# A decode step's recurrent states as the moving operand of their matmuls, with zero-padded queries as weights

## The reference, cut to what matters

```
def step(S, inp):
    qc, kc, vc, gc = inp
    b = jnp.cumsum(gc, axis=1)
    o = jnp.einsum('bthk,bhkv->bthv', qc * jnp.exp(b), S)
    ...
    bl = b[:, -1]
    S = jnp.exp(bl)[..., None] * S + jnp.einsum('bshk,bshv->bhkv', kc * jnp.exp(bl[:, None] - b), vc)
    return S, o
```

## Time and profile before

| | |
|---|---|
| three runs | 2344.84, 2345.38 (median), 2351.37 us |
| profiled execution, own time | 2343.79 us |
| its span in the profile | 2342.0 us |
| busy in the span: PE, PEld, DVE | 2258.5, 2182.4, 1586.0 us |
| busy in the span: ACT, POOL | 654.2, 1225.4 us |
| mean granted clock of TensorE | 0.975 |

### The profile page before, as it was taken

One profiled execution on the slowest core, in us unless ns is written; L12 is line 12 of the kernel. 1 busy time (PEld: TensorE's weight loads), 2 busy tenths in 40 slices (PEclk: granted clock), 3 DMA queues, 4 the chain that ended last, 5 costly groups with the idle time before them and its releaser, 6 DMA issues.

```text
span 2342.0 us, 40326 instructions
## 1 busy us (share of the span) xinstructions
PE 2258.5 (96%) x14908; PEld 2182.4 (93%) x14908; DVE 1586.0 (68%) x4291; ACT 654.2 (28%) x818; POOL 1225.4 (52%) x921
## 2 busy tenths in 40 slices
PE   7999999999999998899999999999999999999997
PEld 7899989898999998899999999999999999999996
DVE  6432723697865477977978978942267777777777
ACT  3212320465111001222223222222233333333332
POOL 4444331254555443777677777770034656565652
PEclk9999997799999999999999999999999999999998
DMA  6345345356998745675344344343588989898973
GB/s 204 108 144 158 117 151 166 122 160 224 306 329 279 244 137 179 178 220 160 106 135 127 112 133 127 116 130 129 220 315 298 319 325 320 317 329 312 330 246 123
DMA packets 294232, 477.57 MB, mean 204 GB/s; under 512 B 32864, under 2 KB 206048, under 8 KB 291824
## 3 DMA queue, kind: packets, MB, share of 16 engines
q1 hardware_dynamic: 202432, 285.84, 38.0%
q10 hardware_dynamic: 54832, 123.04, 14.2%
q0 software_dynamic: 36864, 67.45, 8.6%
HBM read 394.59 MB, written 148.75 MB: 232 GB/s over the span
## 4 chain that ended last, share of the span: by engine, by line
PE 79%; DVE 16%; ACT 1%; issue 1%; DMA 1%; POOL 0%; ACTq 0%; DVEq 0%; SPq 0%; POOLq 0%
PE ps L511 48%; PE ps L761 26%; DVE same L1564 3%; DVE twin L1560 3%; DVE w_lo L1515 2%; PE ps L668 1%; PE ps L613 1%; PE ps L717 1%; PE ps L660 1%; DMA zsa<-sig_scratch 1%; DVE xpad L1346 1%; DVE rstd L1408 0%; PE ps L638 0%; PE ps L550 0%; DVE rr L1396 0%
## 5 line engine op out<-in xcount | busy, mean ns | idle before, releaser
L1515 DVE TENSOR_TENSOR w_lo<-w_raw,w_hi 128x1024 fp32r<-128x1024 f32 x246 | 301.4, 1225 | 350.6 <-ACT w_hi L1035 347.3
L1035 ACT ACTIVATE w_hi<-w_raw 128x1024 fp32r<-128x1024 f32 x246 | 260.7, 1060 | 873.8 <-PE ps L511 583.4
L456 POOL DMA_INDIRECT gate_table<-g_sum,g_idx x384 | 415.5, 1082 | 166.6 <-issue 124.9
L511 PE MATMUL ps<-n_hi,w_hi 128*128 128x288 f32 x2048 | 445.0, 298 | 30.3 <-DVE w_lo L1515 26.1
L511 PE MATMUL ps<-n_lo,w_hi 128*128 128x288 f32 x2048 | 441.2, 297 | 0.0
L511 PE MATMUL ps<-n_hi,w_lo 128*128 128x288 f32 x2048 | 440.6, 296 | 0.0
L435 POOL TENSOR_SCALAR w_hi<-w_raw 128x1024 fp32r<-128x1024 f32 x106 | 126.1, 1190 | 495.1 <-issue 361.6
L761 PE MATMUL ps<-c_hi,w_lo 128*128 128x448 f32 x1024 | 371.7, 363 | 0.0
L761 PE MATMUL ps<-c_lo,w_hi 128*128 128x448 f32 x1024 | 371.2, 362 | 0.0
L761 PE MATMUL ps<-c_hi,w_hi 128*128 128x448 f32 x1024 | 368.9, 360 | 1.0 <-issue 0.8
L511 PEld LDWEIGHTS ps<-n_hi,w_hi 128*128 128x128 f32 x2048 | 332.5, 191 | 34.1 <-DVE w_lo L1515 21.9
(11 more groups left out here) (278 smaller groups left out, 3424.9 us busy)
## 6 DMA issues: line engine op xcount, KB each, us to landing
value_rows<-in_down SPq DMA_DIRECT2D x128, 512.0 KB, 5.5
w_raw<-in_up SPq DMA_DIRECT2D x128, 512.0 KB
w_raw<-in_down SPq DMA_DIRECT2D x128, 512.0 KB
w_raw<-in_trunk SPq DMA_DIRECT2D x96, 512.0 KB
act_scratch<-ast ACTq DMA_DIRECT2D x128, 288.0 KB, 2.1
gate_table<-zeros SPq DMA_DIRECT2D x32, 896.0 KB, 8.1
c_act<-act_scratch ACTq DMA_DIRECT2D x16, 1792.0 KB, 16.3
c_gate<-gate_table ACTq DMA_DIRECT2D x16, 1792.0 KB, 21.9
```

What stands on the lines that cost most here:

```text
L456: nc.gpsimd.indirect_dma_start(g_cells, bass.IndirectOffsetOnAxis(ap=idx, axis=0), gate, None).then_inc(scattered, 16)
L511: last = nc.tensor.matmul(ps[:, 2 * p + a, 0:w], wt[:, k, :], act[:, k, t0 + a * w:t0 + (a + 1) * w], start=k == 0 and part == 0, stop=k = ...
L1035: A(w_hi[j % 2][:, :, :], w_raw[j][:, :, :], ACT.Copy).then_inc(d_hi_done, 1)
L1515: V.tensor_tensor(w_lo[j % 2][:, :, :], w_raw[j][:, :, :], f(w_hi[j % 2][:, :, :]), ALU.subtract).then_inc(d_lo_done, 1)
```

## The change

Operands of the state read change places. For sequence s the weights are now `q_seg`: 128 rows (the key dimension) by 128 columns, zero but for the 8 query columns of this sequence, which stand at column s x 8 for even heads and 64 + s x 8 for odd heads. The moving operand is the state, 256 columns. The 8 sequences and the two heads of a pair accumulate in the same PSUM region, so that after s = 7 two banks hold 128 rows (two heads x 64 tokens) by 256 columns. ACT copies them out (`so`), four PE transposes turn them into bank 6, and DVE adds them to `o`. DVE prepares `q_seg` in two alternating buffers (`q_rows`): clear the columns of s-2, copy those of s. To cover the copy, tile N_GZ is run ahead of the first gate matmuls, and the second half of these waits for `o_norm`.

```diff
+    q_seg = [at(f"q_seg{i}", [P, HEADS, 2 * NSEQ * DEC], F32, g7 + 2368 + 2048 * i) for i in range(2)]
+    so = at("so", [P, HEADS // 2, DV], F32, g7 + 33024)
...
+    qseg_done, so_copied, so_turned = sem("qseg_done"), sem("so_copied"), sem("so_turned")
...
                 pe.wait_ge(gla_in[s % SB], 16 * (s // SB + 1))
-                for g in range(2 * HEADS):
-                    h, d = g // 2, g % 2
-                    t0 = TP + s * DEC
-                    last = nc.tensor.matmul(ps[:, 4, g * 64 + s * DEC:g * 64 + (s + 1) * DEC],
-                                            st_s[s % SB][:, h, d * P:(d + 1) * P], qk[:, h, t0:t0 + DEC],
-                                            start=True, stop=True)
+                pe.wait_ge(qseg_done, s + 1)
+                for h in range(HEADS):
+                    last = nc.tensor.matmul(ps[:, 4 + h // 2, 0:DV], q_seg[s % 2][:, h, :], st_s[s % SB][:, h, :],
+                                            start=s == 0 and h % 2 == 0, stop=s == NSEQ - 1 and h % 2 == 1)
                 last.then_inc(si_done, 1)
...
             pe.wait_ge(s_done, 2 * (CT + NSEQ))
-            pe.wait_ge(o_norm, 1)
             pe.wait_ge(rgw_in, 16 * 3)
             for k in range(KT):
+                if k == 0:
+                    tile(N_GZ)
+                    pe.wait_ge(so_copied, 1)
+                    for g in range(HEADS):
+                        last = nc.tensor.transpose(ps[:, 6, g * P:(g + 1) * P],
+                                                   so[:, g // 2, (g % 2) * P:(g % 2 + 1) * P], idt[:, :])
+                    last.then_inc(so_turned, 1)
                 pe.wait_ge(conv_done, 2 * (k + 1))
...
                 for g in range(2):
+                    if k == 0 and g == 1:
+                        pe.wait_ge(o_norm, 1)
...
-                tile(N_GZ + 2 * k)
+                if k:
+                    tile(N_GZ + 2 * k)
                 tile(N_GZ + 2 * k + 1)
...
+            act.wait_ge(si_done, NSEQ)
+            A(so[:, :, :], ps[:, 4:6, 0:DV], ACT.Copy).then_inc(so_copied, 1)
...
+            def q_rows(s):
+
+                if s > 1:
+                    dve.wait_ge(si_done, s - 1)
+                for hh in range(2):
+                    rows = q_seg[s % 2][:, :, :].rearrange("p (a b) t -> p a b t", b=2)[:, :, hh, hh * 64:(hh + 1) * 64]
+                    if s > 1:
+                        V.memset(rows[:, :, (s - 2) * DEC:(s - 1) * DEC], 0.0)
+                    last = V.tensor_copy(rows[:, :, s * DEC:(s + 1) * DEC],
+                                         qk[:, 0:HEADS, TP + s * DEC:TP + (s + 1) * DEC].rearrange(
+                                             "p (a b) t -> p a b t", b=2)[:, :, hh, :])
+                last.then_inc(qseg_done, 1)
+
+            dve.wait_ge(o_done, CT)
+            for i in range(2):
+                last = V.memset(q_seg[i][:, :, :], 0.0)
+            link(last)
+            q_rows(0)
             for s in range(NSEQ):
+                if s + 1 < NSEQ:
+                    q_rows(s + 1)
...
-            dve.wait_ge(o_copied, CT)
-            V.tensor_tensor(o[:, :, TP:], o[:, :, TP:], ps[:, 4, :].rearrange("p (g t) -> p g t", t=NSEQ * DEC),
-                            ALU.add).then_inc(o_norm, 1)
...
                 if k < KT - 1:
                     taps(k + 1)
+                if k == 0:
+                    dve.wait_ge(o_copied, CT)
+                    dve.wait_ge(so_turned, 1)
+                    turned = ps[:, 6, :].rearrange("p (a d b t) -> p a b d t", a=2, d=2, b=2)
+                    for a in range(HEADS // 2):
+                        rows = o[:, 4 * a:4 * a + 4, TP:].rearrange("p (b d) t -> p b d t", b=2)
+                        last = V.tensor_tensor(rows, rows, turned[:, a, :, :, :], ALU.add)
+                    last.then_inc(o_norm, 1)
```

## The result

The changed kernel took 2328.0 us (median of 4 runs, 2326.63 to 2329.9), the kernel before 2347.52 beside it (4 runs, 2344.84 to 2351.37): ratio 0.9916, 95% interval 0.9898 to 0.9935, so 19.5 us less. The forecast was 2333.5 (11.9 less) in a range of 2329.5 to 2341.5: the sign was right, the size too small, and the median lies 1.5 us under the range. Two later comparisons of the same two kernels gave 15.1 us (0.9942, 0.9927 to 0.9956) and 17.1 us (0.9933, 0.9919 to 0.9947); the recorded ratios are not quotients of the medians, and by them these two gains are 13.6 and 15.7 us. One execution of the kernel before took 2722 us at a mean clock of 0.757 and is left out of every median here.

The account below looks back on a forecast made before the run. The state loop was taken as bound by PE's halved clock; at full clock its last update ends 12.6 us sooner, ACT's gate-loop stage 11.9 sooner. 2345.38 - 11.9 = 2333.5 us, range 2329.5 to 2341.5.

Parts of the forecast that it names:

- the median of the runs is 1.59 above it: Whole kernel: the runs' median lies 1.59 us above the profiled execution, turning 2331.9 into 2333.5 us.
- the 80 rows that stayed: Rival, state loop: the clock still falls, for instance through the updates' 80 rows; 3.8 us slower, about 2349; chance 0.13.
- the gain was not lost behind the gate loop: Denies a rival: gain appears at the gate loop, is lost behind it; within 2 us of 2345; chance 0.05.
- the first, the partial hold: Rival: clock falls at state 6's bare wait and stays low, or `q_rows` costs its upper bound; about 2338.5; chance 0.14.
- The weighed rule: Trainium skill: idle time halves the clock, avoid gaps between matmuls; the prediction did not take it as a full account.
- So DVE sets the cycle: State loop at full clock: a state takes 3.67 us on DVE against 3.59 on PE.
- the 0.4 us for `q_rows`: State loop, DVE ahead of `k_seg`: two clears and two copies cost 0.4 us a state, bounds 0.25 and 0.9.
- the bare `taps(0)`: After state 5: `taps(0)` takes 2.88 us on DVE, uncovered; PE waits about 3 us before state 6's update.
- 2.0 for the clock: State loop after the bare wait: half clock costs 2.0 us, between bounds of nothing and 5.4.
- I cost it at nothing: State transfers: each load lands within about two cycles, 7.3 us, so none delays a state; cost nothing.
- The way out and the first round: Last update to gate products done 10.05 us; then ACT's own work about 9.5, reaching its stage 11.9 us sooner.
- Behind it PE runs without a gap: Behind the gate loop: PE has no gaps, so that stretch takes as long as before.

Follow-up runs that it names:

- the run with three useless products: Kernel before with three useless 512-column matmuls per state added in the state loop, reads unchanged: 2347.02 us, ratio 0.9998.
- the pair of runs with the pieces: The `zsa` and `sr` loads behind the gate loop cut into pieces in order of use: on the kernel before 2343.67 us, on the changed kernel 2330.01.

## Why the prediction was right and wrong

**The step that failed.** The median of 2328.0 lies 5.5 us under the forecast of 2333.5. Of this, 2.0 us are terms of the sum that were mis-sized: the profiled execution was forecast at 2331.9 and took 2329.9. The other 3.5 us are the step "the median of the runs is 1.59 above it": here the median lay 1.9 us under the profiled execution. Both steps are taken up below, after what was right.

**The clock: right.** That the old loop's cost is its clock, and that wide reads hold it, was right. The windows after show it, and the run with three useless products shows that the clock, not the new form, is worth the time. Two rivals fall: the clock did not fall over the 80 rows that stayed, and the gain was not lost behind the gate loop. Of the first, the partial hold, a stretch of 3 to 4 us is left at state 6 in two of the three profiles of the changed kernel (clock 0.57 and 0.65 over 4 us), and none in the other, each time behind a wait of 2.2 to 2.3 us. The weighed rule (idle time halves the clock) is not borne out as a full account: before fell with PE busy throughout, and the run with useless products, just as busy, stayed at 1.00. By that rule alone the fall would have come at that wait only, which is the first rival and not, as I wrote, the second.

The window of the earlier trace rows on the chunk loop ends at 360, where the clock had held. The loop's last chunk, which the change leaves alone, runs from there: reads of 16 columns in turn with products of 80 columns on 80 rows. In before the clock fell in it with PE busy from 360 to 370:

```profile
360.00:370.00 10.00, 10.00 (x47) 8.75 (x46) 1.54 (x4) 1.30 (x2) 0.00 (x0) 0.59 0.84 244
```

The tile ahead of the first read then began at half clock, in the changed kernel too (0.50 from 369 to 373). Which of the two products lowered it is not shown. A second place for such a change may thus lie right ahead of this one; it was not tried.

**The cycle: mis-sized.** "So DVE sets the cycle", 3.67 us, was wrong. Measured is 3.45 to 3.53, twice PE's 1.73 (I had put 1.76 and 1.83), with PE busy for 16.77 of 17 us from 383 to 400. DVE is level with it, not ahead: `k_seg` ended at 383.17, 0.1 us before the update that waits for it. The term that failed is the 0.4 us for `q_rows`; its four operations overlap more than by half:

```profile
382.54 0.15 DVE L1376 COPY q_seg<-qk 128x16 f32<-128x16 f32 x1
382.55 0.07 DVE L1375 MEMSET q_seg<- 128x16 f32 x1
382.62 0.15 DVE L1376 COPY q_seg<-qk 128x16 f32<-128x16 f32 x1
382.63 0.07 DVE L1375 MEMSET q_seg<- 128x16 f32 x1
382.69 0.48 DVE L1395 TENSOR_SCALAR k_seg<-k_nat,segm 80x512 f32<-80x512 f32 x1
```

`k_seg` starts 0.15 us behind the first of them, under my lower bound of 0.25. From update to update that saved 0.15 to 0.21 us, some 1.1 us over the loop.

**State 6: near sum, wrong wait.** I put 2.88 for the bare `taps(0)` and 2.0 for the clock, and cost the state loads at nothing. The read waited 2.2 us for its load, issued at 400.36 and landing 7.89 later, longer than the 7.3 of the earlier trace rows; the taps ran beside that wait. The half clock cost 1.85 (3.58 less 1.73). Together the update of state 6 came 4.1 us late instead of 4.9. The term "I cost it at nothing" is the one that fell; that the sum came out near is luck, as two errors met.

**The way out and the first round: right.** From the end of the last update to that of the gate products 10.05 us were forecast, 10.2 measured (from 415.33 + 1.73 to 427.25); from there to ACT's L894 9.5 and 9.49. The transposes took 0.44 instead of 0.66. From the first read to L894 the forecast was 60.4 (437.5 less 377.13), measured 58.5 (436.74 less 378.23), so 1.9 us of the sum were missing, nearly all from the cycle and state 6. From L884 to the last `y_lo` before took 113.0 us, after 112.9 from L894: as forecast, the block moved as a whole.

**The base and the range: this is what missed.** With every term as measured the sum is 11.9 + 1.9 = 13.8 us, the two profiled executions lie 13.9 us apart to the last `y_lo`, and the pair of runs with the pieces gave 13.7. The 15.1 to 19.5 of the unaltered kernels hold more. The stage behind the gate loop is where it can come from: "Behind it PE runs without a gap" rested on the earlier trace rows, which begin at 612, and the gate loop ends at 562. Between the two PE waited 3.7 and 1.8 us in the profiled execution of before, and there the two executions of before part by 4.6 us. Without the pieces three of five profiles of before and its variants took the longer course there, and two of seven of the changed kernel and its variants. That the shares of the two courses differ so in general is argued from these few profiles. That the excess goes when the course is fixed is likely, not shown: all 93 runs of before and 16 of the changed kernel lie 18.0 us apart in the median, the 23 and 5 runs with the pieces 13.5, and drawn again at random the two differences range over 13.9 to 18.8 and 11.2 to 17.4. The first result's 2328.0 was also a draw of four low runs: 2331.44 and 2330.9, measured later, lie in the forecast's range. The steps that failed are thus "the median of the runs is 1.59 above it", taken as a constant from three runs, and "the range takes the forecast's bounds": the range had no term for the 8 to 10 us by which this kernel's own runs scatter.

## What to carry to other kernels

Where the granted clock is low while PE counts as busy, price a change of operands by the clock it keeps and not by the instructions it saves; a few useless wide products, run once, tell whether the clock is the cause. Read the rows of a stage up to its end: here the last chunk of a loop taken as the example of a held clock had lost it. Before costing a stage as "as long as before", look at two executions of the unaltered kernel: a stage that differs between them by more than the term in question belongs into the range. A transfer that is hidden in a slow loop has to be costed again for the fast one.

## What was not expected of the hardware

Two of DVE's scalings, 1.55 us together elsewhere, took 3.90 us where they met GpSimd's subtraction of 2.77 us, and from that grew two courses of one and the same program, about 4 us apart. What parts them is whether the second product with `sr` begins behind or ahead of that subtraction. The same wait of PE for a load, 2.2 to 2.3 us, was followed by a stretch at half clock in two executions of the changed kernel and by none in a third. In its state loop a load of 512 KB took 7.89 us to land while the DMA engines stood at 0.98 share and 310 GB/s from 400 to 408.
